# Last sum of squares of a head in two rounded TensorE passes, with two filter taps placed earlier on VectorE

## Chip, cores and metric

The kernel runs on one core of one Trainium2 chip. Its time is the device time of one launch in microseconds (us). Three runs of the kernel before took 1233.39, 1232.71 and 1233.92 us; their median, 1233.39 us, is the time before. The profiled execution is a fourth run.

## What is computed

One decoder layer over 512 prompt tokens and 8 x 4 sample tokens (544 columns in all). The work around the change is the mLSTM memory with four heads of 512 value features. Cut to that part, the reference is:

```python
qh, kh, vh, o = ...                       # projections of the normed input, 4 heads
hm, C, n, m = mlstm_scan(qh, kh, vh, ig, lf, C0, n0, m0)
hm = hm * lax.rsqrt(jnp.mean(hm * hm, axis=-1, keepdims=True) + EPS) * g_mh
hm = hm.reshape(B, T, D_M) * jax.nn.sigmoid(o)
y_m = jnp.einsum('btm,md->btd', hm, w_m_out)
```

The mean of `hm * hm` runs over the 512 features of one head. The kernel also computes a depthwise convolution of width 31 over the tokens, a gated merge with an output projection, and an MLP; all of it is in float32.

## The kernel before

Features lie on the 128 partitions, tokens in the columns. All weights come as one stream of chunks of 512 KB: SyncE issues the transfer of a chunk into one of two slots of `wraw` (L419) as soon as VectorE has finished with the chunk that lay there (`lo_done`). ScalarE rounds the chunk to `whi` in the type fp32r (`hi`, L578, and `split_value`, L711), VectorE subtracts to get the remainder `wlo` (`lo`, L1035), and TensorE multiplies in three passes, whi by xhi, whi by xlo and wlo by xhi, each fp32r (`part`). Each engine runs its own written-out list of work, and engines meet at semaphores.

After eight pairs of chunks for the convolution's gate, the four heads run in a loop on every engine (`Fori(0, HEADS)`). Before that loop TensorE transposes a few rows of gate values into the PSUM tile `side` (L1760 to L1762). ScalarE copies them out (`acol`, L690, `wkcol`, L691, and four exponentials `mcol`, L693), VectorE adds up `asmp` (L1211), and TensorE waits for `asmp_ready` and `pool_step` before its first matmul of the loop.

In a head TensorE runs: the products q0, q1, k0, k1 (chunks 0 to 3 of the head), with two inserted groups `sample_values` that read the raw value chunks in `wraw` (chunks 4 and 5, later 6 and 7) and need both slots landed; the values, the scores, the products of o, and then the stage `pv`. In `pv`, for each of four feature tiles k, TensorE makes the weighted value sum (`weighted`, float32), ScalarE squares it into one half of `sqh` (`weighted_square`, L788), and VectorE multiplies the sum into `hm` (L1393, L1400 for the last) and adds the square to `sqacc` (L1398). Between these stand `update`s of the sample memory (L1370) and convolution taps (L1248; one tap is two instructions, one for each of the head's two channel tiles). How many taps stand behind which tile is written in `PV_TAPS`.

A head ends like this. TensorE: `new_state`, the transposed `hs` (the rows `side<-sel,hs`), and the last sum, a float32 matmul of `ones` with `sqacc` over 512 columns, which adds the squares up over the partitions (the rows `side<-sqacc,ones`), with `ss_ready`. ScalarE: logarithm and exponential of that sum (L815, L817), then a wait for the last tap (`conv_sum`), four copies of the convolution's result (L823, L824), and, in the next turn, `split(3)` (L578, then L1035 on VectorE). The lo part of `split(3)` sets the second slot of `wraw` free, and SyncE issues the transfer of value chunk 5 of the next head (L419), for which the first `sample_values` of that head waits. VectorE goes from the last tap to small products and the scaling of `hm` (L1410, L1417), and then to `split(3)`.

```python
def state_out(half): ...
weighted_square(2)
weighted_square(3)
state_out(1)
act.wait_ge(ss_ready, h + 1)
```

Of the kernel before, what the change touches and what calls it, by code (L numbers as in the profile page):

```python
# [12 lines left out]
P = 128  # L13
D_MODEL = 1024
KT = D_MODEL // P
SEQ = 512
# [17 lines left out]
VT, QT = DV // P, DK // P  # L34
# [60 lines left out]

V_TAPS = [(6, 9), (9, 11)]
O_TAPS = [(14, 16), (16, 16), (16, 22), (22, 24)]
PV_TAPS = [(24, 25), (25, 26), (26, 27), (27, 27)]
UPDATES = [(4, 5), (6,), (), (7,)]
SHARE = EPS * DV / P  # L100
CAP = SHARE * 1e36
# [23 lines left out]
def hybrid_layer(nc, xT, wstream, w_gates, cols, b_gates, b_v, w_dw, hist, c_in, n_in, m_in,  # L125
                 yT, conv_p, conv_s, c_p, n_p, m_p, c_s, n_s, m_s):
    f32, f32r = mybir.dt.float32, mybir.dt.float32r
    ALU = mybir.AluOpType
    ACT = mybir.ActivationFunctionType
# [4 lines left out]
    with ctx:  # L134
        cursor = [4224]

        def at(name, shape, dt, where=None):

            size = 4
            for n in shape[1:]:  # L140
                size *= n
            size = (size + 31) // 32 * 32
            where_ = cursor[0] if where is None else where
            t = nc.alloc_sbuf_tensor_at(name, shape, dt, offset=where_)
            if where is None:
                cursor[0] += size
            assert max(cursor[0], where_ + size) <= 229344, (name, cursor[0])
            return t
# [6 lines left out]
        col = at("col", [P, N_COLS], f32)  # L155
        wdw = at("wdw", [P, KT, WIDTH], f32)
        ones = at("ones", [P, P], f32)
        ident = at("ident", [P, P], f32)
        causal = at("causal", [P, P], f32)
        causal_s = at("causal_s", [NS, DEC_B, DEC_T], f32)  # L160
# [53 lines left out]
        sq2 = at("sq2", [P, 2, TT], f32, tmp0)  # L214
        sg = at("sg", [P, TT], f32, cursor[0])
        sqh = at("sqh", [P, 2, SEQ], f32)
        swin = at("swin", [P, DEC_B, DEC_T, WIDTH], f32, cursor[0] - 2 * SEQ * 4)
        sqacc = at("sqacc", [P, SEQ], f32)
        qm = at("qm", [P, QT, DEC_B * NS], f32)
# [42 lines left out]
        side = ctx.enter_context(nc.psum_tensor("side", [P, 4, 512], f32))  # L262
# [9 lines left out]
        def sem(name):  # L272
            return ctx.enter_context(nc.semaphore(name))
# [36 lines left out]
        srec_ready, conv_sum, conv_copied = sem("srec_ready"), sem("conv_sum"), sem("conv_copied")  # L310
        snum_ready, hs_ready, hs_sq, hs_var, hs_std, hs_norm, hst_ready, hst_used = (sem(n) for n in (
            "snum_ready", "hs_ready", "hs_sq", "hs_var", "hs_std", "hs_norm", "hst_ready", "hst_used"))
        hsq_ready, hsum_ready, ss_ready, var_ready, std_ready = (sem(n) for n in (
            "hsq_ready", "hsum_ready", "ss_ready", "var_ready", "std_ready"))
        kl_ready, kst_ready = sem("kl_ready"), sem("kst_ready")
# [21 lines left out]
        def tile(buf, j, lo=0, n=TT):  # L337

            return buf[:, bass.ds(j, 1), lo:lo + n]
# [232 lines left out]
        def _(act):  # L572
# [121 lines left out]

            act.wait_ge(const_in, 32)
            act.wait_ge(pool_step, 24)
            with act.Fori(0, HEADS) as h:
                def use(name):
                    return wait_filled(act, h, name)
# [84 lines left out]
                def weighted_square(k):  # L784
                    s = use(f"pv{k}")
                    if k >= 2:
                        act.wait_ge(hsum_ready, VT * h + (k - 1))
                    act.activation(sqh[:, k % 2, :], psum[s][:, 0, :], ACT.Square).then_inc(hsq_ready, 1)  # L788

                def state_out(half):  # L790
                    act.wait_ge(cc_ready, 2 * h + (half + 1))
                    act.activation(cst[:, 2 * half:2 * half + 2, :].rearrange("p a k -> p (a k)"), side[:, half, :],
                                   ACT.Copy).then_inc(cst_ready, 1)
# [15 lines left out]
                state_out(0)  # L809
                weighted_square(2)  # L810
                weighted_square(3)
                state_out(1)

                act.wait_ge(ss_ready, h + 1)
# [209 lines left out]
        def _(dve):  # L1024
            V = nc.vector
# [195 lines left out]
            with dve.Fori(0, HEADS) as h:  # L1221
# [12 lines left out]
                def taps(first, last):  # L1234

                    for tap in range(first, last):
                        for q in range(2):
                            w = wdw[:, bass.ds(2 * h + q, 1), tap].rearrange("p a -> p (a)")
                            src = tile(u, 2 * h + q, tap, SEQ)
                            sum_ = accp[:, q:q + 1, :]  # L1240
                            if tap == 0:
                                ins = V.tensor_scalar(sum_, src, w, c("b_dw", 2 * h + q), ALU.mult, ALU.add)
                            else:
                                if tap > first:
                                    dve.wait_ge(dve_step, conv_at[q])
                                elif q == 0:
                                    dve.wait_ge(dve_step, conv_at[1])
                                ins = V.scalar_tensor_tensor(sum_, src, w, sum_, ALU.mult, ALU.add)  # L1248
                            if tap == WIDTH - 1:
                                ins.then_inc(conv_sum, 1)  # L1250
                            else:
                                conv_at[q] = mark(ins)
# [114 lines left out]
                def update(n):  # L1367
                    s = use(f"cu{n}")
                    b = ORDER[n]
                    V.scalar_tensor_tensor(crg[:, n % C_RING, :, :], crg[:, n % C_RING, :, :], hb[:, R_DEC + b:R_DEC + b + 1],  # L1370
                                           psum[s][:, :, :], ALU.mult, ALU.add).then_inc(drained[s], 1)
# [16 lines left out]
                for k in range(VT):  # L1388
                    s = USES.index(f"pv{k}") % 2
                    dve.wait_ge(hsq_ready, VT * h + (k + 1))  # L1390
                    d = tile(hm, 4 * h + k, 0, SEQ)
                    if k < VT - 1:
                        V.tensor_tensor(d, d, psum[s][:, 0:1, :], ALU.mult).then_inc(drained[s], 1)  # L1393
                    if k >= 1:
                        dve.wait_ge(hsum_ready, VT * h + k)
                    else:
                        dve.wait_ge(d_ready, h + 1)
                    V.tensor_tensor(sqacc[:, :], sqacc[:, :], sqh[:, k % 2, :], ALU.add).then_inc(hsum_ready, 1)  # L1398
                    if k == VT - 1:
                        V.tensor_tensor(d, d, psum[s][:, 0:1, :], ALU.mult).then_inc(drained[s], 1)  # L1400
                    for n in UPDATES[k]:
                        update(n)
                    taps(*PV_TAPS[k])
                taps(27, WIDTH - 1)
# [254 lines left out]
        def _(pe):  # L1659
            def mm(out, lhsT, rhs, start, stop, check=False):  # L1660
                return pe.matmul(out, lhsT, rhs, start=start, stop=stop, skip_group_check=check)  # L1661
# [102 lines left out]

            pe.wait_ge(asmp_ready, 1)
            pe.wait_ge(pool_step, 24)
            with pe.Fori(0, HEADS) as h:
                def use(name):
                    n = USES.index(name)
                    free(n % 2, USES_HEAD * h + (S_HEAD + n // 2))  # L1770
                    return n % 2
# [160 lines left out]
                for k in range(VT):  # L1932
                    ins = mm(side[:, 3, NS * k:NS * (k + 1)], hs[:, P * k:P * (k + 1)], sel[:, :], True, True)
                ins.then_inc(hst_ready, 1)
                pe.wait_ge(hsum_ready, VT * h + VT)
                pe.wait_ge(np_used, h + 1)
                mm(side[:, 2, :], ones[:, :], sqacc[:, :], True, True).then_inc(ss_ready, 1)

            def alternate(i, k, c0, s0, xhi, xlo, arrive=None):

# [206 lines left out]
```

## Time and profile before

| | us |
|---|---|
| median of three runs | 1233.39 |
| the profiled execution's own time | 1233.06 |
| its span, first to last instruction | 1231.3 |
| TensorE busy in the span | 1223.1 (99%) |
| VectorE busy | 731.9 (59%) |
| ScalarE busy | 508.2 (41%) |
| GpSimd busy | 65.5 (5%) |

The granted TensorE clock was 1.000 of full speed over the span, and 99.02 MB came over SyncE's queue at 23.8% of the 16 DMA engines' time. TensorE's busy time counts from the start of one matmul to its modelled end, and neighbours overlap, so short losses are read from the starts of the matmuls and from idle times ahead of them. Of VectorE and ScalarE only that part matters for which something on TensorE waits.

### The profile page before, as it was taken

The numbers are of one execution on the slowest core, as the hardware profiler recorded it, in microseconds if no ns is written. First come the engines' busy times: TensorE is split into PE (matmuls) and PEld (weight loads), VectorE is DVE, ScalarE is ACT, GpSimd is POOL, SyncE is SP. The second block draws the span as 40 slices with busy tenths as digits, with TensorE's granted clock in tenths as the row PEclk, the third lists the DMA queues.
The fourth block names the chain that finished last, engine by engine and source line by source line (L and its number), as shares of the span: only waits on it lengthen the run. The fifth ranks groups of instructions, "written<-read, shape, count | busy, mean of one in ns | idle before, by whom it ended". The sixth has DMA issues, their size and how long they took to land.

```text
span 1231.3 us, 23581 instructions
## 1 busy us (share of the span) xinstructions
PE 1223.1 (99%) x9103; PEld 1153.5 (94%) x9103; DVE 731.9 (59%) x1031; ACT 508.2 (41%) x783; POOL 65.5 (5%) x129
## 2 busy tenths in 40 slices
PE   9999999999999999999999999999999999999998
PEld 9999878989787898979999999999999999999998
DVE  6933788888888888887455434338543112443334
ACT  7533433353454335335443212246654223454222
POOL 4020001101100110110000000000000000000000
PEclk9999999999999999999999999999999999999999
DMA  6353225516432551623222222331232222222222
GB/s 221 103 168 137 69 79 216 194 34 238 165 118 83 215 190 34 238 104 103 87 90 98 74 98 85 141 104 57 98 102 87 85 96 75 85 90 97 86 68 73
DMA packets 40341, 141.23 MB, mean 115 GB/s; under 512 B 4788, under 2 KB 7220, under 8 KB 40168
## 3 DMA queue, kind: packets, MB, share of 16 engines
q1 hardware_dynamic: 28456, 99.02, 23.8%
q0 software_dynamic: 11424, 41.23, 9.5%
q8 instruction: 32, 0.52, 0.2%
q10 hardware_dynamic: 416, 0.35, 0.1%
q14 instruction: 13, 0.11, 0.0%
HBM read 118.31 MB, written 22.26 MB: 114 GB/s over the span
## 4 chain that ended last, share of the span: by engine, by line
PE 94%; DMA 2%; DVE 1%; issue 1%; ACT 1%; DVEq 0%; ACTq 0%; SPq 0%
PE product L1661 85%; PE side L1661 9%; DMA wraw<-in_wstream 2%; DVE wlo L1035 1%; ACT whi L711 0%; PE side L1846 0%; DVE accp L1248 0%; ACT whi L578 0%; ACT L578 0%; DVE crg L1370 0%; DVE qn L1291 0%; DVE sqacc L1398 0%; PE side L1836 0%; DVEq L1248 0%; DVE hm L1400 0%
## 5 line engine op out<-in xcount | busy, mean ns | idle before, releaser
L1035 DVE TENSOR_TENSOR wlo<-wraw,whi 128x1024 fp32r<-128x1024 f32 x176 | 214.8, 1224 | 209.1 <-ACT whi L578 188.3
L1661 PE MATMUL product<-ahi,whi 128*128 128x256 f32 (+1 forms) x1392 | 294.0, 290 | 1.2 <-DVE asmp L1211 1.2
L1661 PE MATMUL product<-ahi,wlo 128*128 128x256 f32 (+1 forms) x1392 | 290.2, 288 | 0.0
L1661 PE MATMUL product<-alo,whi 128*128 128x256 f32 (+1 forms) x1392 | 287.9, 286 | 0.0
L578 ACT ACTIVATE whi<-wraw 128x1024 fp32r<-128x1024 f32 x160 | 167.7, 1052 | 209.8 <-PE product L1661 148.2
L1661 PEld LDWEIGHTS product<-ahi,whi 128*128 128x128 f32 x1392 | 223.7, 188 | 11.5 <-issue 10.5
L1661 PEld LDWEIGHTS product<-alo,whi 128*128 128x128 f32 x1392 | 224.0, 188 | 0.0
L1661 PEld LDWEIGHTS product<-ahi,wlo 128*128 128x128 f32 x1392 | 222.8, 188 | 0.0
L1248 DVE SCALAR_TENSOR_TENSOR accp<-u,wdw,accp 128x512 f32<-128x512 f32 x240 | 163.6, 743 | 0.7 <-DVE accp L1248 0.7
L1661 PE MATMUL product<-hidhi,whi 128*128 128x288 f32 (+1 forms) x512 | 111.2, 289 | 0.0
L1661 PE MATMUL product<-hidlo,whi 128*128 128x288 f32 (+1 forms) x512 | 111.0, 288 | 0.0
L1661 PE MATMUL product<-hidhi,wlo 128*128 128x288 f32 (+1 forms) x512 | 110.4, 286 | 0.0
L1661 PEld LDWEIGHTS product<-hidlo,whi 128*128 128x128 f32 x512 | 84.1, 188 | 0.1
L1661 PEld LDWEIGHTS product<-hidhi,wlo 128*128 128x128 f32 x512 | 83.8, 189 | 0.0
L1661 PEld LDWEIGHTS product<-hidhi,whi 128*128 128x128 f32 x512 | 83.4, 188 | 0.1
L1569 DVE TENSOR_TENSOR hidlo<-fr,hidhi 128x544 f32 (+1 forms) x32 | 23.2, 726 | 74.9 <-ACT hidhi L952 74.9
L1661 PE MATMUL product<-whi,ahi 128*128 128x512 f32 (+1 forms) x160 | 56.8, 355 | 0.0
L1661 PE MATMUL product<-wlo,ahi 128*128 128x512 f32 (+1 forms) x160 | 55.8, 348 | 0.0
L1661 PE MATMUL product<-whi,alo 128*128 128x512 f32 (+1 forms) x160 | 55.7, 348 | 0.0
L1661 PE MATMUL product<-bhi,whi 128*128 128x256 f32 (+1 forms) x256 | 55.6, 288 | 0.0
L1661 PE MATMUL product<-bhi,wlo 128*128 128x256 f32 (+1 forms) x256 | 55.4, 287 | 0.0
L1661 PE MATMUL product<-blo,whi 128*128 128x256 f32 (+1 forms) x256 | 55.2, 287 | 0.0
(320 smaller groups left out, 1755.3 us busy)
## 6 DMA issues: line engine op xcount, KB each, us to landing
wraw<-in_wstream SPq DMA_DIRECT2D x176, 512.0 KB, 3.5
crg<-in_c_in POOLq DMA_DIRECT2D x32, 512.0 KB, 6.5
out_c_s<-crg POOLq DMA_DIRECT2D x32, 512.0 KB, 3.2
hb<-head_rows POOLq DMA_DIRECT2D x4, 580.0 KB, 5.3
x<-in_xT SPq DMA_DIRECT2D x4, 544.0 KB, 6.4
sgm<-in_xT SPq DMA_DIRECT2D x1, 2176.0 KB, 8.1
out_c_p<-cst POOLq DMA_DIRECT2D x4, 512.0 KB, 8.1
out_yT<-y SPq DMA_DIRECT2D x4, 288.0 KB, 2.2
```

The costliest lines, as they stand in the source:

```text
L578: act.activation(whi[:, k % RING, :, :], wraw[:, k % 2, :, :], ACT.Copy).then_inc(hi_done, 1)
L1035: V.tensor_tensor(wlo[:, k % RING, :, :], wraw[:, k % 2, :, :], whi[:, k % RING, :, :].bitcast(f32), ALU.subtract).then_inc(lo_done, 1)
L1248: ins = V.scalar_tensor_tensor(sum_, src, w, sum_, ALU.mult, ALU.add)
L1569: V.tensor_tensor(tile(hidlo, j), fr[:, 2 + b:3 + b, :], tile(hidhi, j).bitcast(f32), ALU.subtract).then_inc(hid_lo, 1)
L1661: return pe.matmul(out, lhsT, rhs, start=start, stop=stop, skip_group_check=check)
```

## The change

A tile `ones_r` is `ones` in fp32r. ScalarE makes it once, by a copy that stands after the four exponentials `mcol` and ahead of its head loop, and TensorE waits for it (`unit_ready`) ahead of its own head loop. In each head the last sum is no longer one float32 matmul: ScalarE copies `sqacc` rounded to fp32r into `sqr[:, 0]`, VectorE subtracts to get the remainder `sqr[:, 1]`, and TensorE adds both over the partitions in two fp32r matmuls into the same PSUM columns, each behind a wait of its own. `sqr` lies where `sqh` lies. `PV_TAPS` moves tap 25 from tile 1 to tile 0 and tap 26 from tile 2 to tile 1; the number of taps stays.

```diff
-PV_TAPS = [(24, 25), (25, 26), (26, 27), (27, 27)]
+PV_TAPS = [(24, 26), (26, 27), (27, 27), (27, 27)]
@@
+        ones_r = at("ones_r", [P, P], f32r)
+        sqr = at("sqr", [P, 2, SEQ], f32r, cursor[0] - 2 * SEQ * 4)
@@ scalar, ahead of the loop over the heads
             act.wait_ge(pool_step, 24)
+            act.activation(ones_r[:, :], ones[:, :], ACT.Copy).then_inc(unit_ready, 1)
@@ scalar, in a head
                 weighted_square(3)
+                act.wait_ge(hsum_ready, VT * h + VT)
+                act.activation(sqr[:, 0, :], sqacc[:, :], ACT.Copy).then_inc(hsum_hi, 1)
                 state_out(1)
@@ vector, in a head
                     if k == VT - 1:
                         V.tensor_tensor(d, d, psum[s][:, 0:1, :], ALU.mult).then_inc(drained[s], 1)
+                        dve.wait_ge(hsum_hi, h + 1)
+                        V.tensor_tensor(sqr[:, 1, :], sqacc[:, :], sqr[:, 0, :].bitcast(f32), ALU.subtract).then_inc(hsum_lo, 1)
@@ tensor, ahead of the loop over the heads
             pe.wait_ge(pool_step, 24)
+            pe.wait_ge(unit_ready, 1)
@@ tensor, in a head
-                pe.wait_ge(hsum_ready, VT * h + VT)
                 pe.wait_ge(np_used, h + 1)
-                mm(side[:, 2, :], ones[:, :], sqacc[:, :], True, True).then_inc(ss_ready, 1)
+                pe.wait_ge(hsum_hi, h + 1)
+                mm(side[:, 2, :], ones_r[:, :], sqr[:, 0, :], True, False)
+                pe.wait_ge(hsum_lo, h + 1)
+                mm(side[:, 2, :], ones_r[:, :], sqr[:, 1, :], False, True).then_inc(ss_ready, 1)
```

## Rows read from the trace of the kernel before

**Rows 1.** The page, chain that ended last: share of the span by line.

```profile
PE product L1661 85%; PE side L1661 9%; DMA wraw<-in_wstream 2%; DVE wlo L1035 1%; ACT whi L711 0%; PE side L1846 0%; DVE accp L1248 0%; ACT whi L578 0%; ACT L578 0%; DVE crg L1370 0%; DVE qn L1291 0%; DVE sqacc L1398 0%; PE side L1836 0%; 
```

**Rows 2.** Timeline of TensorE, 111 to 113: start, length, work, count, [idle before <- releaser].

```profile
111.43 0.16 PE L1762 MATMUL side<-ident,rout 4*32 4x4 f32 x1
112.79 0.38 PE L1661 MATMUL product<-ahi,whi 128*128 128x256 f32 x1 [1.20 <-DVE asmp L1211]
```

**Rows 3.** Chain of waits, 105 to 120: start, length, what it went through.

```profile
112.47 0.32 issue
```

**Rows 4.** Timeline of ScalarE, 112 to 116, ahead of the head loop and into it.

```profile
112.62 1.28 ACT L693 ACT_TABLE_LOAD   x1
113.92 0.72 ACT L693 ACTIVATE mcol<-side 32x4 f32<-32x4 f32 x4
114.66 1.28 ACT L578 ACT_TABLE_LOAD   x1
```

**Rows 5.** Groups of ScalarE by form: count | busy, mean ns of one.

```profile
L743 ACT ACTIVATE kwh<-kws 32x256 fp32r<-32x256 f32 x4 | 1.7, 418 | 0.1
```

**Rows 6.** Timeline of TensorE, end of the first head.

```profile
217.01 1.89 PE L1661 MATMUL side<-kw,vtok 128*128 128x256 f32 x8
218.74 0.97 PE L1661 MATMUL side<-sel,hs 128*128 128x32 f32 x8
219.55 1.10 PE L1661 MATMUL side<-sqacc,ones 128*128 128x512 f32 x2
```

**Rows 7.** Chain of waits, 117 to 160: 48 fp32r value passes of 512 columns.

```profile
146.71 11.12 PE product L1661 x48
```

**Rows 8.** Timeline of VectorE, stage pv of the first head.

```profile
210.98 0.69 DVE L1393 TENSOR_TENSOR hm<-hm,product 128x512 f32 x1 [1.30 <-ACT sqh L788]
...
216.53 1.41 DVE L1248 SCALAR_TENSOR_TENSOR accp<-u,wdw,accp 128x512 f32<-128x512 f32 x2
217.86 0.68 DVE L1398 TENSOR_TENSOR sqacc<-sqacc,sqh 128x512 f32<-128x512 f32 x1
...
219.06 1.27 DVE L1370 SCALAR_TENSOR_TENSOR crg<-crg,hb,product 128x1024 f32<-128x1024 f32 x1
```

**Rows 9.** Timeline of ScalarE, the last square of the first head.

```profile
216.74 0.60 ACT L788 ACTIVATE sqh<-product 128x512 f32<-128x512 f32 x1 [1.56 <-PE product L1661]
```

**Rows 10.** Timelines of VectorE, ScalarE and SyncE, last tap to the next value chunk.

```profile
224.49 1.41 DVE L1248 SCALAR_TENSOR_TENSOR accp<-u,wdw,accp 128x512 f32<-128x512 f32 x2 [0.18 <-DVE accp L1248]
...
226.07 0.63 ACT L823 ACTIVATE u<-accp 128x512 f32 x1 [4.03 <-DVE accp L1248]
...
230.06 1.23 DVE L1035 TENSOR_TENSOR wlo<-wraw,whi 128x1024 fp32r<-128x1024 f32 x1 [0.88 <-ACT whi L578]
...
231.45 0.33 SPq L419 DMA_DIRECT2D wraw<-in_wstream  x1
```

**Rows 11.** First `sample_values` of heads two, three, four on TensorE (timeline).

```profile
235.54 1.07 PE L1661 MATMUL side<-wraw,asmp 128*32 128x256 f32 x16
...
343.05 1.07 PE L1661 MATMUL side<-wraw,asmp 128*32 128x256 f32 x16
...
451.15 1.07 PE L1661 MATMUL side<-wraw,asmp 128*32 128x256 f32 x16 [0.39 <-DMA wraw<-in_wstream]
```

**Rows 12.** Line L419 in 229 to 233 and in 336.5 to 341: landing of each transfer.

```profile
DMA to landing us min/median/max: 3.5/3.5/3.5
...
L419 SPq DMA_DIRECT2D wraw<-in_wstream  x1: 332/332/332, 339.0 to 339.0; - x1
...
DMA to landing us min/median/max: 3.8/3.8/3.8
```

**Rows 13.** Tile side on TensorE, 1.4 to 5.7 and 5.9 to 7.3: ns min/median/max.

```profile
L1661 PE MATMUL side<-ones x20: 421/421/581, 1.3 to 5.6; 128*128 128x128 f32 x20
...
L1661 PE MATMUL side<-ones x13: 274/275/421, 5.6 to 7.1; 128*128 128x128 f32 x13
```

More of the change, by code:

```diff
@@ L312, in hybrid_layer @@
             "snum_ready", "hs_ready", "hs_sq", "hs_var", "hs_std", "hs_norm", "hst_ready", "hst_used"))
+        unit_ready = sem("unit_ready")
+        hsum_hi, hsum_lo = sem("hsum_hi"), sem("hsum_lo")
         hsq_ready, hsum_ready, ss_ready, var_ready, std_ready = (sem(n) for n in (
```

## The prediction

> **What bounds the kernel now.** I read the chain that ended last first: 94% of it is TensorE, and the only other link of any size is the transfer of weights into `wraw`, 2% [rows 1]. So a microsecond counts only if TensorE starts its next matmul later or earlier by it. Then I looked at the three places that the change touches: where TensorE enters the head loop, the end of a head, and the first group of the next head that waits for a transfer.
>
> At the entry of the loop TensorE stands still from 111.59 (111.43 + 0.16) to 112.79 [rows 2]. It waits for `asmp`, and from that tile's end to the first product 0.32 pass [rows 3]. ScalarE at that time is late: it loads a table at 112.62, makes the four exponentials from 113.92, and has finished with them at about 114.66, where the load of its loop begins [rows 4]. Nothing on TensorE waits for that today.
>
> At the end of a head TensorE does not wait: the matmuls of `hs` follow `new_state` at 218.74, and the last sum follows at 219.55 [rows 6]. Behind the head lies a chain off TensorE: last tap on VectorE ends at 225.90 (224.49 + 1.41), ScalarE copies from 226.07, lo part of chunk 3 on VectorE at 230.06, transfer of a value chunk issued at 231.45 [rows 10]. ScalarE waits 4.03 for the tap and VectorE 0.88 for ScalarE, so the last tap sets this chain. `sample_values` needs what it brings. In head two the chunk lands at 234.95 (231.45 + 3.5) and TensorE comes at 235.54; in head three it lands at 342.8 (339.0 + 3.8) and TensorE comes at 343.05; in head four TensorE waits 0.39 for it [rows 10 to 12].
>
> **The change part by part.** All sums are against the profiled execution, 1233.06, which lies 0.33 below the median 1233.39; the forecast is moved up by that. A measurement of this kernel tells about 0.2%, 2.5 us, from no change.
>
> *The two passes.* A float32 matmul appears as two records; eight of 256 columns take 218.74 - 217.01 = 1.73, so 0.216 each and 0.43 for 512 columns [rows 6]. The sum costs 2 x 0.43 = 0.86. An fp32r pass of 512 columns costs 11.12 / 48 = 0.232 [rows 7]; two cost 0.46. TensorE gains 0.40 at each head's end. Less if the second pass comes late or its weights are loaded behind the wait: I take 0.35, bounds 0.20 and 0.45.
>
> *The waits in front of them, and the taps.* The last square ends at 217.34 (216.74 + 0.60) [rows 9], but the addition starts at 217.86, behind the taps of tile 2 that start at 216.53 [rows 8]. With these taps gone it starts at about 217.40. The moved pair needs about 1.33 (217.86 - 216.53), and finds room: VectorE stood idle for 1.30 ahead of tile 1, so that tile starts as before; behind tile 1 one pair replaces another [rows 8]. The addition ends at 218.08, ScalarE's copy of 512 columns (0.60, as the square in rows 9) at about 218.72, the product into `hm` is done at 218.68, and VectorE subtracts from about 218.8 to 219.5. TensorE reaches the first pass at 219.55 and the second 0.23 later: neither wait holds it. `state_out(1)` stands behind the new copy on ScalarE and is delayed by little, and nobody on the path waits for it.
>
> *What VectorE pays.* The subtraction starts at 218.8 and the next instruction 0.60 later (an instruction of 0.68 is followed after 219.06 - 217.86 = 1.20 for two), at 219.40, where `update` started at 219.06 [rows 8]: 0.34 late. Handovers between engines take up to 0.17 (225.90 to 226.07) [rows 10]; there are three. So the last tap, and with it the whole chain to the value chunk, is 0.3 to 0.9 late; I take 0.40, near the row that gives the starts. GpSimd's stores and loads of the sample memory shift with `update` by the same; the scaling of `hm` follows the taps and ends well within VectorE's 0.88 idle plus the shift of ScalarE.
>
> *Where the gain meets the delay.* I let TensorE start `sample_values` 0.1 after the landing (0.2 at most, or head three would show idle time), so the slack is 235.54 - 235.05 = 0.49, 343.05 - 342.9 = 0.15 and 0 [rows 11, 12]. The shift at each is the larger of -0.35 and 0.40 less the slack: -0.09, +0.25, +0.40. After head four no such group follows and the gain stays: -0.35. Sum +0.21; with the bounds -0.2 (delay 0.3, gain 0.45) and +1.9 (delay 0.9, gain 0.20). The second `sample_values` hangs on the first and moves with it.
>
> *The copy `ones_r`.* It stands behind the exponentials on ScalarE, TensorE's wait for it stands ahead of the loop, and the whole of the first head is queued behind that wait. The copy can start at 114.66 [rows 4]. A copy of 256 columns takes 0.42 [rows 5]; this one has 128; I take 0.31, bounds 0.2 and 0.42. It ends at 114.97, and with the same 0.32 to the first product TensorE starts at 115.29 instead of 112.79: **+2.50**, bounds 2.4 and 2.6. This is paid once, and nothing gives it back: TensorE is the bound behind it, and the transfers of head one are gated by what it finishes. Split 3 on ScalarE is 0.3 late and has many microseconds until its chunk is used.
>
> Whether the table load comes ahead of the copy is open. The trace has a load of 1.28 right ahead of a plain copy, at 114.66 [rows 4]. That load would make the stall 3.78. But it belongs to the first instruction of the loop, and the new copy stands outside. The Trainium skill, ScalarE: Activation LUTs, section "Table sets: the hidden batching unit", says that copy is in every set, so that no load is needed; by it the stall is 2.50, by the row taken plainly 3.78.
>
> Total +2.50 + 0.21 = +2.7: 1235.8 for a profiled execution, **1236.1** for the median. This case's own range is 1235.6 to 1237.9 (2.4 - 0.2, 2.6 + 1.9).
>
> **The rivals.** (a) *The clock falls in the stall.* TensorE would stand idle from 111.59 to 115.29, 3.7 instead of 1.2. The granted clock was 1.000, the 2.4 GHz level, all through, with the idle of 1.2 in it. But the first matmuls after the launch took 421 ns, later ones of the same shape 275, and the slow ones lasted from 1.3 to 5.6 [rows 13]. If it falls to 1.2 GHz in the stall and stays there for as long, 4.3 at half pace lose 2.15: 1238.3. Against it: nothing in this trace shows a fall after idling. The Trainium skill, TensorE: Matmul & The Clock Gate, section "HAM oscillation — how this bites in real kernels", says that matmuls start cold again after waits that leave the engine idle long enough; by that rule this case would be the likely one, and its time the 1238.3 above.
>
> (b) *The load comes first*: stall 3.78, total +4.0, 1237.4.
>
> (c) *The chunks land in time.* If the delayed transfers are not later than TensorE in heads two to four (handovers short, and landing at 3.5 and less each time), each head gives 0.35 to 0.40, four give 1.4 to 1.6, and with the stall the sum is +1.0: 1234.4, no measurable change. For it: the transfer before head two has slack. Against it: in head four TensorE waits already.
>
> (d) *Not slower: the stall is not there.* It decides at one place, the entry of the loop: if the copy is done by 112.47, where `asmp` ends, the price is 0 and only +0.2 is left: 1233.6; with (c) besides, 1231.9. That needs ScalarE to make the copy ahead of its exponentials. The program puts it behind them and ScalarE runs in order, so I give it little. It would also hold if TensorE's wait weren't on the way, as when the change did not do what it says.
>
> **How the numbers follow.** Main case 0.60, (a) 0.12, (b) 0.08, (c) 0.12, (d) 0.08. The bound for slower is 1235.86. The main case's value lies just above it; I count two thirds of it, 0.42, as slower, the rest as same. With (a) and (b) slower has 0.62; same has 0.18 + 0.12 + 0.05 = 0.35; faster 0.03, from (d) with (c), which reaches below 1230.9 only with noise. The range runs from 1234.2, taking in (c), to 1238.5, taking in (a) and (b); left out are (d) and the far ends.
>
> **What would show it.** In the profile after: TensorE's idle ahead of its first product of the loop grows from 1.20 to 3.7, released by ScalarE's copy, which is there once; the copy starts at 114.7 without a load ahead of it; `side<-sqr,ones_r` has eight records starting 0.23 apart; the addition of tile 3 in head one starts 0.4 earlier relative to the last square, the subtraction at its place, and `update` 0.3 to 0.5 later relative to TensorE; TensorE waits for `wraw` in heads two to four, 0.5 to 0.8 in the fourth. I am wrong if the first product starts near 112.8, if the matmuls behind the stall take 421 ns, or if the waits for `wraw` stay as they are while the last tap comes late.

## The result, and the profile after

The changed kernel took 1238.43 us in the median of six runs (1237.42 to 1240.13), the kernel before 1232.90 in six runs beside it. The ratio is 1.0047, with a 95% interval of 1.0037 to 1.0057: slower by 5.5 us at the medians, 4.6 to 7.0 by the interval. The forecast was 1236.1, or 2.7 us slower; the time came out inside the range, 0.07 below its upper end (1238.5), at twice the forecast loss. The profiled execution took 1238.80, its span 1237.3.

The page's head and its slices. In the second block each digit is a fortieth of the span; the granted clock, 9 in every slice before, has one 8.

```profile
span 1237.3 us, 23598 instructions
...
PE 1225.3 (99%) x9103; PEld 1156.1 (93%) x9103; DVE 734.9 (59%) x1035; ACT 510.7 (41%) x788; POOL 65.3 (5%) x129
...
PEclk9998999999999999999999999999999999999999
```

The timeline of TensorE at the entry of the head loop, which answers to [rows 2]: start, length, work, count, idle and who ended it.

```profile
111.52 0.16 PE L1771 MATMUL side<-ident,rout 4*32 4x4 f32 x1
115.50 0.82 PE L1670 MATMUL product<-ahi,whi 128*128 128x256 f32 x2 [3.82 <-ACT ones_r L701]
116.12 0.66 PE L1670 MATMUL product<-alo,whi 128*128 128x256 f32 x2
...
120.65 0.66 PE L1670 MATMUL product<-ahi,wlo 128*128 128x256 f32 x2
121.10 0.47 PE L1670 MATMUL product<-ahi,whi 128*128 128x256 f32 x2
121.41 0.41 PE L1670 MATMUL product<-alo,whi 128*128 128x256 f32 x2
121.65 0.41 PE L1670 MATMUL product<-ahi,wlo 128*128 128x256 f32 x2
```

Two things are to be seen. The idle time of 1.20 is now 3.82, released by the copy of `ones_r`. And the matmuls behind it start 0.45 apart in pairs (120.65 to 121.10), where they start 0.25 apart later (121.41 to 121.65 is 0.24). The windows of the same stretch, with the granted clock in the last but two column, say why: it is 0.55 and 0.60 of full speed, a mixture of the 1.2 and the 2.4 GHz level. The last row, a window inside the idle time, has 0.50: the clock had fallen to the 1.2 GHz level before any matmul behind the stall ran. In windows of a quarter and half a microsecond it is 1.00 up to 114.25, 0.77 in the next quarter, and back at 1.00 from 121.5 (0.79 in 121.0 to 121.5), so it was low from about 114.4 to 121.2.

```profile
110.00:114.00 4.00, 1.68 (x18) 1.44 (x16) 1.24 (x3) 1.73 (x7) 1.36 (x4) 1.00 0.28 107
114.00:118.00 4.00, 2.50 (x11) 2.51 (x12) 0.54 (x1) 3.87 (x9) 0.49 (x1) 0.55 0.66 277
118.00:122.00 4.00, 4.00 (x22) 4.00 (x22) 0.68 (x1) 1.43 (x5) 0.00 (x0) 0.60 0.38 131
122.00:126.00 4.00, 4.00 (x34) 4.00 (x33) 1.51 (x3) 0.00 (x0) 0.00 (x0) 1.00 0.00 0
...
114.50:115.50 1.00, 0.00 (x0) 0.01 (x1) 0.00 (x0) 0.94 (x4) 0.00 (x0) 0.50 0.87 361
```

ScalarE in the same stretch, where [rows 4] stood. The copy follows the exponentials without a table load; the load still belongs to the loop.

```profile
114.00 0.72 ACT L697 ACTIVATE mcol<-side 32x4 f32<-32x4 f32 x4
114.75 0.31 ACT L701 ACTIVATE ones_r<-ones 128x128 fp32r<-128x128 f32 x1
115.07 1.28 ACT L582 ACT_TABLE_LOAD   x1
```

The sum of it, from starts in the two profiled executions: the first product starts at 115.50 instead of 112.79, 2.71 later (0.09 of that was there before the entry, since the idle time grew by 2.62). The first `sample_values` of head one starts at 133.23 instead of 127.96, 5.27 later; the difference, 2.56, is the slow stretch. The span ends 6.0 later, so the four heads and the step into the next stage add 0.75.

The end of the first head, where [rows 6, 8, 9] stood: TensorE, VectorE and ScalarE. The `hs` matmuls lie 5.13 later than before (223.87 - 218.74), and this is the shift taken off below.

```profile
223.87 0.97 PE L1670 MATMUL side<-sel,hs 128*128 128x32 f32 x8
224.68 0.71 PE L1670 MATMUL side<-sqr,ones_r 128*128 128x512 f32 x2
225.29 0.51 PE L1670 MATMUL product<-ahi,whi 128*128 128x256 f32 x2
225.64 0.41 PE L1670 MATMUL product<-alo,whi 128*128 128x256 f32 x2
```

```profile
222.50 0.69 DVE L1405 TENSOR_TENSOR sqacc<-sqacc,sqh 128x512 f32<-128x512 f32 x1 [0.75 <-ACT sqh L793]
223.11 0.68 DVE L1407 TENSOR_TENSOR hm<-hm,product 128x512 f32 x1
223.89 0.69 DVE L1409 TENSOR_TENSOR sqr<-sqacc,sqr 128x512 fp32r<-128x512 f32 x1
224.50 1.28 DVE L1377 SCALAR_TENSOR_TENSOR crg<-crg,hb,product 128x1024 f32<-128x1024 f32 x1
```

```profile
221.87 0.60 ACT L793 ACTIVATE sqh<-product 128x512 f32<-128x512 f32 x1 [1.56 <-PE product L1670]
223.23 0.63 ACT L818 ACTIVATE sqr<-sqacc 128x512 fp32r<-128x512 f32 x1 [0.76 <-DVE sqacc L1405]
```

Taken back by 5.13, the last addition starts at 217.37 (forecast 217.40), the copy at 218.10, the subtraction at 218.76 (218.8) and `update` at 219.37 (219.40, before 219.06). The gain of the two passes is read from the matmul behind the first pair of the next product: from the `hs` matmuls to `alo,whi` it is now 1.77 (225.64 - 223.87). Before, that row started 1.99 after 218.74 [rows 6]:

```profile
220.73 0.41 PE L1661 MATMUL product<-alo,whi 128*128 128x256 f32 x2
```

So the gain at the end of the first head is 0.22. Read in the same way the ends of the other heads give 0.32, 0.30 and 0.40 (from 2.00 each to 1.68, 1.70 and 1.60), 1.24 in all. Most of it is given back a few microseconds later. The first matmul of the product `k0` writes into the PSUM slot of `q0` and waits until VectorE has copied that slot to `qT`; this copy stands behind the lo part of `split(3)`, and so at the end of the chain behind the last tap. The weight loads of TensorE (PEld) show a wait for it in heads two, three and four, which the kernel before doesn't have:

```profile
237.48 0.30 PEld L1670 LDWEIGHTS product<-ahi,whi 128*128 128x128 f32 x2 [0.18 <-DVE qT L1276]
...
PEld product L1670 <- DVE qT L1276: 0.7, 3, 0.3
```

By the starts of the matmuls there (in head two 0.38 and 0.36 apart instead of 0.25) TensorE loses 0.24, 0.32 and 0.30, about as much as it had gained at the three head ends before them.

The waits of TensorE over the whole span, in us in total, times, and the longest:

```profile
PE product L1670 <- ACT ones_r L701: 3.8, 1, 3.8
PE side L1670 <- DMA wraw<-in_wstream: 1.9, 5, 0.5
...
PE product L1670 <- ACT sgm L841: 0.5, 1, 0.5
PE product L1670 <- DVE wlo L1042: 0.5, 1, 0.5
```

The waits for value weights are as before in total (before 1.8 in 5). Only one of the five stands ahead of the first `sample_values` of a head, 0.48 in head two; the other four stand ahead of the second group. The wait for `sgm` is new: 0.54 in the gate products behind the last head. The one for `wlo` lies in the first 40 us, ahead of all that was changed.

### The profile page after: what moved, and what is told of

Read it like the earlier page. It is cut to its first block, busy times and chain, and to the rows that moved or that the text cites. A ratio compares the mean times of both kernels' runs of the same rounds, so it can differ in the third digit from the quotient of the medians.

```text
span 1237.3 us, 23598 instructions
## 1 busy us (share of the span) xinstructions
PE 1225.3 (99%) x9103; PEld 1156.1 (93%) x9103; DVE 734.9 (59%) x1035; ACT 510.7 (41%) x788; POOL 65.3 (5%) x129
## 4 chain that ended last, share of the span: by engine, by line
PE 92%; DMA 2%; DVE 2%; ACT 2%; issue 1%; DVEq 0%; ACTq 0%; SPq 0%
PE product L1670 83%; PE side L1670 9%; DMA wraw<-in_wstream 2%; DVE accp L1255 1%; DVE wlo L1042 1%; ACT whi L716 0%; DVE crg L1377 0%; PE side L1856 0%; ACT whi L582 0%; ACT L582 0%; DVE sqacc L1405 0%; DVE hm L1426 0%; ACT sqr L818 0%; ACT sqh L793 0%; DVEq L1255 0%
```

## The experiments

Theory S: the stall at the entry and the lower clock behind it make up nearly the whole loss. Its rivals put the loss at the heads' ends, or the slow stretch down to something else than the idle time. Theory G is about the other half of the change: why it brings nothing even without the stall. Every time stands against the kernel before, measured beside it.

**Making `ones_r` early.** The tile is copied ahead of the third group of gate products.

```diff
+            act.activation(ones_r[:, :], ones[:, :], ACT.Copy).then_inc(unit_ready, 1)
             glu(2, {1: (gate_weights,)})
@@
             act.wait_ge(pool_step, 24)
-            act.activation(ones_r[:, :], ones[:, :], ACT.Copy).then_inc(unit_ready, 1)
```

> The changed kernel with one line moved: ScalarE makes ones_r ahead of the third group of gate products, when nothing waits for it, instead of behind the four exponentials. Theory S (the stall at the entry of the head loop of 2.7 us, and the lower TensorE clock behind it, which costs 2.5 more, make up nearly the whole loss; the heads' ends give and take about nothing): TensorE's idle ahead of its first product of the loop goes back to 1.2 us, the granted clock is 1.000 in every stretch, and the time falls by 5.2 to within 1 us of the kernel before. Rival H (the loss lies in the heads' ends, in the transfers of value weights that come late, and shows only together with the rest): the time stays 2 us or more above the kernel before.

Measured: 1233.28 against 1232.88, ratio 1.0006 (0.9997 to 1.0015), the mean clock 1.000 in all 11 runs. The copy now runs at 65.16, and the entry and the clock look as before:

```profile
112.94 0.51 PE L1670 MATMUL product<-ahi,whi 128*128 128x256 f32 x2 [1.20 <-DVE asmp L1218]
...
114.00:118.00 4.00, 4.00 (x34) 4.00 (x33) 0.81 (x1) 3.89 (x10) 0.55 (x2) 1.00 0.66 277
```

One line moved takes 5.15 us away (1238.43 - 1233.28, with the kernel before at 1232.90 and 1232.88 beside them). The loss lies in where this copy stands, and the rest of the change is worth nothing that can be measured.

**The wait alone.** The kernel before, with `ones_r`, its copy behind the exponentials and the wait, the sum left as it was.

```diff
+        ones_r = at("ones_r", [P, P], f32r)
@@
+            act.activation(ones_r[:, :], ones[:, :], ACT.Copy).then_inc(unit_ready, 1)
@@
+            pe.wait_ge(unit_ready, 1)
```

> The kernel before with nothing but the tile ones_r, its copy behind the exponentials and TensorE's wait for it; the last sum stays one float32 matmul on ones, and ones_r is not used. Theory S: the first product starts 2.7 us later, its matmuls are at half pace until about 5.5 us later, and the time is 5.2 us above the kernel before (bounds 4 to 6.5, since the clock may come back earlier or later). Rival: a wait of this length costs itself alone, 2.7 us.

Measured: 1237.10 against 1232.88, 4.2 above it and inside the bounds 4 to 6.5, though under the 5.2 named; ratio 1.0040 (1.0026 to 1.0053). The stall is the same, and a slow stretch follows it:

```profile
115.86 0.82 PE L1664 MATMUL product<-ahi,whi 128*128 128x256 f32 x2 [3.82 <-ACT ones_r L699]
...
114.00:118.00 4.00, 2.14 (x9) 2.15 (x10) 0.18 (x1) 3.86 (x9) 0.85 (x2) 0.51 0.66 277
118.00:122.00 4.00, 4.00 (x24) 4.00 (x23) 1.04 (x1) 1.78 (x5) 0.00 (x0) 0.63 0.37 129
```

The first `sample_values` of head one starts 5.33 later than before. Of that 0.45 was there ahead of the entry, 2.62 is the longer idle time, and 2.26 is the slow stretch. At the end of the span 4.3 is left, and the waits for the value weights are 0.8 in all instead of 1.8. A loss of 2.7 alone, the rival, would need less than the interval allows (its lower end is 3.2).

**The idle time filled.** The changed kernel, with TensorE kept at work up to `ones_r`.

```diff
+            for _ in range(15):
+                mm(side[:, 2, 0:P], ones[:, :], ones[:, :], True, True)
             pe.wait_ge(asmp_ready, 1)
```

> The changed kernel with fifteen float32 matmuls of ones with ones, 128 columns, into an unused part of side, ahead of the wait for asmp. They take 0.22 us each, 3.3 in all, so TensorE works in the time in which it stood idle, and is done when ones_r is. Theory S: the first product still starts near 115.5, but at the full clock; the time is 2.5 us below the changed kernel and 2.7 to 3 above the one before. Rival C (the half pace behind the stall is not the idle time's doing but comes from the first products themselves or their weights): the matmuls behind the wait are slow as before, and the time is that of the changed kernel.

```profile
111.64 3.62 PE L1670 MATMUL side<-ones 128*128 128x128 f32 x30
115.54 0.51 PE L1670 MATMUL product<-ahi,whi 128*128 128x256 f32 x2 [0.28 <-issue]
115.89 0.41 PE L1670 MATMUL product<-alo,whi 128*128 128x256 f32 x2
...
114.00:118.00 4.00, 3.72 (x32) 3.54 (x31) 0.50 (x1) 3.86 (x10) 0.53 (x2) 1.00 0.66 277
```

The product starts at 115.54, as in the changed kernel, and at full clock: the idle time makes the clock fall, not the products, as the window at 0.50 ahead of the first product says too. Head one's first `sample_values` comes 2.72 later than before, the stall without the slow stretch. The time was a partial miss: 1237.19 against 1232.88, ratio 1.0037 (1.0025 to 1.0049), only 1.2 below the changed kernel. Four of the six runs had a mean clock of 1.000 and took 1235.62 to 1237.47; two had 0.998 and took 1238.83 and 1239.58. Where the clock fell in those two was not profiled. In the profiled run the heads added 1.4 more, with waits of 0.56 for `hm` and 0.71 for a chunk that the kernel before does not have; why they came here stays open.

**A shorter stall.** The copy ahead of the exponentials and their table load.

```diff
+            act.activation(ones_r[:, :], ones[:, :], ACT.Copy).then_inc(unit_ready, 1)
             for j in range(QUAD):
                 act.activation(mcol[NS * j:NS * (j + 1), :], side[0:NS, 3, 24:28], ACT.Exp, scale=-1.0).then_inc(rowT_used, 1)
@@
-            act.activation(ones_r[:, :], ones[:, :], ACT.Copy).then_inc(unit_ready, 1)
```

> The changed kernel with the copy of ones_r ahead of the four exponentials and their table load. The copy then ends near 112.97 and TensorE's first product of the loop starts near 113.3, 0.4 to 0.5 late, with 1.7 us idle instead of 3.8. Theory S: the clock stays at 1.000 there and the time is 0.4 above ones_r made early, 1233.7. Rival: a somewhat longer idle time than before is enough for the clock to fall, and the time is 2 us or more above it.

Measured: 1233.48 against 1232.31, ratio 1.0013 (1.0004 to 1.0022). TensorE stood idle for 1.64 and the clock stayed at 1.00 in the profiled run, as expected. That is 1.2 above the kernel before at the medians, where `ones_r` made early was 0.4 above it. Not every run kept the clock: eight of the eleven had a mean of 1.000 and took 1232.89 to 1233.73, three had 0.998 or 0.999 and took 1235.03 to 1235.45. Where it fell in these three was not profiled.

```profile
113.18 0.51 PE L1670 MATMUL product<-ahi,whi 128*128 128x256 f32 x2 [1.64 <-ACT ones_r L696]
```

**The taps alone.** The kernel before with the new `PV_TAPS`.

```diff
-PV_TAPS = [(24, 25), (25, 26), (26, 27), (27, 27)]
+PV_TAPS = [(24, 26), (26, 27), (27, 27), (27, 27)]
```

> The kernel before with the new PV_TAPS alone. Theory S: the last tap, and the chain behind it to the next head's value chunk, is 0.45 us earlier, so the waits for wraw ahead of the first sample_values go, and with them at most 0.4 us in all; the time is 0 to 1 us below the kernel before, which a measurement cannot tell from it. Rival H: the new order costs something by itself, 0.5 us or more at each head, so 2 us above.

Measured: 1232.22 against 1232.88, ratio 0.9995 (0.9986 to 1.0004): no measurable difference, as expected. The first `sample_values` of a head no longer waits in its trace; the second one still does, 1.4 in 4 instead of 1.8 in 5.

**The two passes without the taps.** `ones_r` early, the old `PV_TAPS`.

```diff
-PV_TAPS = [(24, 26), (26, 27), (27, 27), (27, 27)]
+PV_TAPS = [(24, 25), (25, 26), (26, 27), (27, 27)]
```

> The kernel with ones_r made early and the old PV_TAPS, so the two passes without the moved taps. Theory G: the addition of tile 3 starts 0.4 us later than with the taps moved, the subtraction and the last tap come later by as much, the second pass waits for the subtraction by about 0.1 to 0.3, and each first sample_values and the gate products come 0.4 later: 1 to 1.8 us above ones_r made early, 1234.7. Rival: the taps have no part in it, and the time is 1233.3.

Measured: 1235.12 against 1232.31, ratio 1.0022 (1.0013 to 1.0031), so slower, by 2.8 at the medians. That is more than expected: against `ones_r` made early, 0.4 above the kernel before, it is 2.4 where 1 to 1.8 were named. The taps have a part: without their move the subtraction starts only at 219.65, and TensorE waits between the passes. The two take 0.93 instead of 0.71, and from the `hs` matmuls to `alo,whi` it is 2.19 (221.34 - 219.15), 0.20 more than the float32 sum had.

```profile
219.15 0.97 PE L1670 MATMUL side<-sel,hs 128*128 128x32 f32 x8
219.96 0.93 PE L1670 MATMUL side<-sqr,ones_r 128*128 128x512 f32 x2
...
221.34 0.42 PE L1670 MATMUL product<-alo,whi 128*128 128x256 f32 x2
...
219.65 0.69 DVE L1409 TENSOR_TENSOR sqr<-sqacc,sqr 128x512 fp32r<-128x512 f32 x1
```

**One tap more taken out of the way.** `ones_r` early, and the pair of tap 24 ahead of `pv`, so that one pair less stands behind the last addition.

```diff
-O_TAPS = [(14, 16), (16, 16), (16, 22), (22, 24)]
-PV_TAPS = [(24, 26), (26, 27), (27, 27), (27, 27)]
+O_TAPS = [(14, 16), (16, 16), (16, 22), (22, 25)]
+PV_TAPS = [(25, 27), (27, 28), (28, 28), (28, 28)]
@@
-                taps(27, WIDTH - 1)
+                taps(28, WIDTH - 1)
```

> The kernel with ones_r made early, and one more tap taken out of the stretch behind the last addition: O_TAPS ends with (22, 25), PV_TAPS is (25, 27), (27, 28), (28, 28), (28, 28), and 28 to 30 stand behind. Theory G (the gain of the two passes at each head's end, 0.3 to 0.4 us, is given back because the chain last tap, ScalarE's copies, split 3, transfer, sample_values is already as late as TensorE): the last tap now comes 1.3 us earlier against the kernel with ones_r early, no first sample_values waits for wraw, the wait of 0.54 in the gate products behind the last head goes, and the time is 1.2 to 2 us below the kernel before (1231.3). Rival N (the gain was never there, because the passes and their waits cost what the float32 matmul cost): the time stays at that of ones_r made early, 1233.3.

Measured: 1231.36 against 1232.31, ratio 0.9991 (0.9982 to 1.0000), 0.95 below it where 1.2 to 2 were expected. ScalarE's copy of the convolution starts at 225.20, where it started at 226.07 [rows 10], and the waits for `sgm` and for `qT` are gone. No first `sample_values` waits; the four waits for value weights that are left stand ahead of the second group:

```profile
225.20 0.64 ACT L830 ACTIVATE u<-accp 128x512 f32 x1 [3.41 <-DVE accp L1255]
...
PE side L1670 <- DMA wraw<-in_wstream: 1.3, 4, 0.4
PE product L1670 <- DVE wlo L1042: 0.4, 1, 0.4
```

Theory G had the giving back right and its place wrong. With `ones_r` early alone the first `sample_values` of heads two to four don't wait either. What waits there is `k0`, for `qT`, as in the changed kernel:

```profile
PEld product L1670 <- DVE qT L1276: 0.8, 3, 0.3
```

And the value chunk isn't there sooner by the extra tap: in head two it is issued at 230.57 instead of 231.90 and takes 4.7 instead of 3.4, so that it lands at 235.3 in both; in heads three and four it is the same to 0.2. Why the transfer takes longer when it is issued earlier stays open. The two waits that the extra tap took away, 0.8 for `qT` and 0.5 for `sgm`, are what lies between the two kernels: one is 0.40 above the kernel before, the other 0.95 below it.

The same taps without the two passes:

> The kernel before with the taps of the first kernel of this call alone: float32 sum, O_TAPS ending with (22, 25), PV_TAPS (25, 27), (27, 28), (28, 28), (28, 28). Theory G: the chain is early, the waits of the first sample_values go, 0.4 to 0.8 us below the kernel before (1232.3), and 1.0 to 1.6 above the same taps with the two passes. Rival N: both tap orders give the same with and without the passes.

Measured: 1232.34 against 1232.31, ratio 0.9998 (0.9989 to 1.0007). The gain of 0.4 to 0.8 over the kernel before did not come; of the 1.0 to 1.6 between this kernel and the one with the passes, 0.98 came at the median (1232.34 - 1231.36). In the traces of the two the passes save 0.27, 0.32, 0.31 and 0.40 at the four head ends, 1.3 in all. So the passes bring about 1 us once VectorE's `qT` comes early enough, and the taps by themselves bring nothing.

**Both once more.**

> The kernel with ones_r early and one more tap moved, once more, to see whether its 0.95 us below the kernel before holds. Theory G: 0.5 to 1.5 us below the kernel before again, with an interval that ends at or below 1. Rival: that was the spread of the runs, and it comes out within 0.3 us of it.

Measured: 1231.63 against 1232.74, ratio 0.9991 (0.9982 to 1.0000): 1.1 below again. Twice, in 11 runs each time, this kernel lies 1 us below the one before, with intervals that just reach 1. It is the best version found, and beats the changed kernel by 6 to 7 us.

> The changed kernel itself beside it, to see how its runs spread. Theory S: every run has a clock below 1.000, since the idle time of 3.8 us is in each, and 5 to 6 us above the kernel before in the median; the runs with the lower mean clock are the longer ones, 1 us for each 0.001. Rival: the fall of the clock is a matter of chance, and some runs keep 1.000 and are only 2.7 to 3.5 us above.

Measured: 1237.61 against 1232.74, ratio 1.0046 (1.0032 to 1.0059), 4.9 above it where 5 to 6 were expected. All five runs had a mean clock below 1.000 (0.997 to 0.999), as had all six of the first measurement (0.996 to 0.999), and all five of the kernel with the wait alone. Of the 70 runs of the kernel before that stand beside the experiments, six did (0.998 or 0.999). So the fall comes with the idle time. How long the clock stays low differs from run to run. In this profile the matmuls are back at full pace at 118.30, 2.9 after the first product, instead of 5.6:

```profile
117.87 0.60 PE L1670 MATMUL product<-ahi,wlo 128*128 128x256 f32 x2
118.30 0.41 PE L1670 MATMUL product<-ahi,whi 128*128 128x256 f32 x2
118.55 0.42 PE L1670 MATMUL product<-alo,whi 128*128 128x256 f32 x2
```

One microsecond for each 0.001 did not hold (0.999 with 1237.61, 0.997 with 1237.59).

## Why the prediction was right or wrong

*The copy `ones_r`.* Right in place, cause and size. Its duration was put at 0.31 and took 0.31; the stall at 2.50, measured 2.62. The first product comes 0.44 after the copy's end (115.50 - 115.06), not 0.32 as after `asmp`, which is the 0.1 too little. On the table load row and rule spoke against each other: the load before a plain copy in [rows 4], and the sentence of the Trainium skill, ScalarE: Activation LUTs, section "Table sets: the hidden batching unit", that copy is in every set. The trace after agrees with the rule; no load stands ahead of the copy.

*The step that failed: "(a) The clock falls in the stall" was left a rival with a chance of 0.12, and the main sum ran at full clock.* In the main sum the fall of the clock stood at nothing; the runs showed it in every run of the changed kernel, at 2.56 us in the profiled one. As a rival the prediction had the idle time right (3.7, measured 3.82), the price nearly (2.15, measured 2.56) and the resulting time (1238.3, measured 1238.43). That the time agrees to 0.1 is in part luck: the second profile of the same kernel pays 1.3 for the clock, and the heads cost 0.75 instead of 0.21. What it gave too little to was the case itself, on the ground that nothing in the trace of before shows a fall after idling. That was no ground: the trace had no idle time of such a length behind the warm start, so it could neither show nor exclude it, and the one row that spoke at all, slow matmuls after the launch [rows 13], spoke for it. The Trainium skill, TensorE: Matmul & The Clock Gate, section "HAM oscillation — how this bites in real kernels", spoke for it as well, and the runs agree: all eleven runs of the changed kernel had a clock below full, and with the idle time filled the products behind the same wait ran at full pace.

*The two passes.* 0.35 was forecast; 0.22, 0.32, 0.30 and 0.40 were measured at the four head ends, all inside the bounds 0.20 to 0.45, with a mean of 0.31. At the first head's end the second pass starts not 0.23 but about 0.3 after the first, and the first weight load of the next product comes late: in the trace 0.33 of idle time stand ahead of it that no semaphore ended.

```profile
224.65 0.30 PEld L1670 LDWEIGHTS side<-sqr,ones_r 128*128 128x128 f32 x2
225.28 0.30 PEld L1670 LDWEIGHTS product<-ahi,whi 128*128 128x128 f32 x2 [0.33 <-issue]
```

My reading is that TensorE's sequencer is held at the wait for `hsum_lo` and so does the branch of the loop late. The traces bear it out in part: such idle time stands ahead of that weight load at the three ends where the loop turns (0.33, 0.24, 0.27) and not at the fourth, where it ends and the gain is the full 0.40 that the two costs in the prediction differ by. That the wait has a part in it was not tried; the kernel before shows 0.24 twice at the same place, behind its float32 passes.

*What VectorE pays.* Right: `update` was forecast 0.34 late by the starts and is 0.31 late. The taps do what was said: tile 1 starts as before and the last addition 0.49 earlier (forecast 0.46), and without them the passes lose time.

*Where the gain meets the delay.* Right that the gain is given back, and wrong on where. The shifts of the first `sample_values` from head to head were forecast as -0.09, +0.25, +0.40. Measured they are 0.42 (5.69 - 5.27), 0.23 (5.92 - 5.69) and -0.50 (5.42 - 5.92). The transfers did not repeat their landing times (3.5, 3.8 and 4.4 us before, 4.2, 3.5 and 3.8 after), so that TensorE waited 0.48 ahead of the first `sample_values` in head two and not at all in heads three and four, where 0.5 to 0.8 were forecast for the fourth. The prediction let VectorE's delay reach TensorE by the value chunk alone. It reaches it earlier, at `k0`, which waits for `qT`, and there the gain of the head end before is gone in heads two to four, whether or not the chunk is late. The second `sample_values`, which was to move with the first, has waits of its own, before (0.23 to 0.44) and after (0.17 to 0.53). One sentence was wrong as well: "After head four no such group follows and the gain stays". The gate products wait 0.54 for `sgm`, which ScalarE makes after the last scaling of `hm` on VectorE, so the 0.40 of the fourth head is given back there. In all, the heads were put at +0.21; in the trace they are +0.75, and by the kernel with `ones_r` early the whole change without the stall is +0.4 (-0.4 to +1.8 by its interval).

*The rivals.* (b), the load first, did not occur. (c), chunks in time, came true in heads three and four without its gain, since `k0` waits for `qT`; with one more tap moved the passes bring 1.0, where 1.4 to 1.6 were said. (d) did not occur; the copy stands behind the exponentials in the trace as in the program. In the chances two thirds of 0.60 were put at 0.42; they are 0.40, which changes nothing.

## What to carry to other kernels

A one-time constant is not free because it is made once: what counts is what stands ahead of it on its engine's list and who waits for it. Made in a stretch where that engine idled, at 65.16, it cost nothing that could be measured here. When a change lets TensorE stand idle for longer than any gap in the trace so far, price the fall of the clock into the forecast, not as a rival; here it added 1.3 to 2.6 us to a stall of 2.6. And a saving on the bound engine stays only if the chains that it meets next are shortened with it. To find them, list everything that the bound engine takes from the delayed engine, copies that free a PSUM slot too, and not only the one that waits today.

## What the runs showed that I had not expected

The mean clock was below 1.000 in every run of the kernels with 3.8 to 3.9 us of idle time. The clock fell in no profile with 1.2 to 1.6, but three of the eleven runs with 1.64 had a lower mean clock and took at least 1.5 us longer than the median. How long it stayed low differed between two profiles of one kernel: it was back 5.6 and 2.9 us after the first product. That makes the loss 1.3 to 2.6 us and spreads the runs of such a kernel. A float32 matmul of ones with ones was enough to keep the clock up in the profiled run, but in two of six runs of that kernel the mean clock was still 0.998.
